# A two-layer decoder trunk: q, k and y1 transposed by VectorE in 32x32 blocks with a trip through DRAM, and the rotation moved from GpSimd to VectorE

## What is computed

```python
def moba_layer(x, norm_g, w_in, q_norm, k_norm, w_out):
    h = rms_norm(x, norm_g)
    q, k, v, z = jnp.split(h @ w_in, 4, axis=-1)
    q = rope(rms_norm(heads(q), q_norm))
    k = rope(rms_norm(heads(k), k_norm))
    v = heads(v)
    o = moba_attention(q, k, v).transpose(0, 2, 1, 3).reshape(B, S, D_INNER)
    return x + (o * jax.nn.silu(z)) @ w_out
```

## Time and profile before

| | us |
|---|---|
| median of 3 runs | 431.96 (431.88 to 432.15) |
| profiled execution | 431.83 |
| its span | 430.0 |
| PE busy | 423.4 (98%) |
| DVE busy | 284.7 (66%) |
| ACT busy | 231.0 (54%) |
| POOL busy | 131.1 (30%) |
| DMA moved | 75.25 MB, 175 GB/s |

### The profile page before, as it was taken

How to read it: one execution, slowest core, us unless ns; L and a number is a source line. 1 busy time by engine, 2 the same in 40 slices (tenths; PEclk the granted TensorE clock), 3 DMA queues, 4 the chain that set the end, 5 groups by cost and what they waited for, 6 DMA issues and landing times.

```text
span 430.0 us, 5669 instructions
## 1 busy us (share of the span) xinstructions
PE 423.4 (98%) x2214; PEld 362.7 (84%) x2214; DVE 284.7 (66%) x354; ACT 231.0 (54%) x406; POOL 131.1 (30%) x97
## 2 busy tenths in 40 slices
PE   8999999999999999999999999999999999999997
PEld 8979898988888888888788888888888888888885
DVE  3868898779885544356664798447983579836532
ACT  5743653535454443578448765477654786546310
POOL 0078000000000000089904595055940559300000
PEclk9999999999999999999999999999999999999999
DMA  8987669563655747336833667236672355731002
GB/s 260 386 298 241 209 219 365 190 201 122 197 194 173 219 134 221 125 89 214 292 99 99 185 183 228 91 100 193 196 215 84 101 191 195 243 110 39 2 0 98
DMA packets 38026, 75.25 MB, mean 175 GB/s; under 512 B 1648, under 2 KB 1776, under 8 KB 38000
## 3 DMA queue, kind: packets, MB, share of 16 engines
q1 hardware_dynamic: 37280, 73.83, 53.1%
q10 hardware_dynamic: 720, 1.07, 0.8%
HBM read 73.84 MB, written 1.05 MB: 174 GB/s over the span
## 4 chain that ended last, share of the span: by engine, by line
PE 85%; POOL 7%; DMA 2%; DVE 2%; SPq 1%; ACT 1%; issue 1%; DVEq 0%
PE acc L579 23%; PE acc L581 22%; PE acc L580 22%; PE aux L634 4%; POOL wide L326 3%; PE acc L624 3%; PE acc L623 3%; PE acc L621 3%; DMA raw<-in_w_in_dram 2%; PE aux L718 2%; POOL k_s L319 1%; PE aux L725 1%; SPq L232 1%; PE aux L736 1%; PE aux L737 1%; PE aux L717 1%
## 5 line engine op out<-in xcount | busy, mean ns | idle before, releaser
L816 DVE TENSOR_TENSOR w_lo<-raw,w_hi 128x2048 fp32r<-128x2048 f32 x65 | 160.1, 2469 | 54.9 <-ACT w_hi L349 54.8
L349 ACT ACTIVATE w_hi<-raw 128x2048 fp32r<-128x2048 f32 x64 | 122.1, 1917 | 36.7 <-PE acc L581 25.7
L579 PE MATMUL acc<-w_hi,hT_hi 128*128 128x512 f32 x320 | 127.8, 399 | 1.0 <-DVE w_lo L816 1.0
L581 PE MATMUL acc<-w_hi,hT_lo 128*128 128x512 f32 x320 | 124.9, 390 | 0.0
L580 PE MATMUL acc<-w_lo,hT_hi 128*128 128x512 f32 x320 | 124.6, 389 | 0.0
L579 PEld LDWEIGHTS acc<-w_hi,hT_hi 128*128 128x128 f32 x320 | 60.1, 188 | 12.9 <-DVE w_lo L816 1.4
L581 PEld LDWEIGHTS acc<-w_hi,hT_lo 128*128 128x128 f32 x320 | 60.0, 188 | 12.9
L580 PEld LDWEIGHTS acc<-w_lo,hT_hi 128*128 128x128 f32 x320 | 60.2, 188 | 11.7
L579 PE MATMUL acc<-w_hi,aT_hi 128*128 128x512 f32 x160 | 63.7, 398 | 0.0
L581 PE MATMUL acc<-w_hi,aT_lo 128*128 128x512 f32 x160 | 62.4, 390 | 0.0
L580 PE MATMUL acc<-w_lo,aT_hi 128*128 128x512 f32 x160 | 62.3, 389 | 0.0
(11 more groups left out here) (125 smaller groups left out, 569.7 us busy)
## 6 DMA issues: line engine op xcount, KB each, us to landing
raw<-in_w_in_dram SPq DMA_DIRECT2D x46, 1024.0 KB, 5.4
raw<-in_w_out_dram SPq DMA_DIRECT2D x16, 1024.0 KB, 5.0
raw<-in_w_pool_dram SPq DMA_DIRECT2D x4, 1024.0 KB, 5.7
raw<-in_w_in_dram SPq DMA_DIRECT2D x8, 256.0 KB, 7.5
wide<-in_xT_dram ACTq DMA_DIRECT2D x4, 256.0 KB, 7.0
xs<-in_x_dram SPq DMA_DIRECT2D x1, 1024.0 KB, 7.8
out_dram<-ysb SPq DMA_DIRECT2D x4, 256.0 KB, 2.1
wide<-in_table_dram SPq DMA_DIRECT2D x1, 256.0 KB, 9.0
```

The costliest lines, as they stand in the source:

```text
L349: act.activation(w_hi[:, slot, :], raw[:, slot, :], ACT.Copy).then_inc(hi_made, 1)
L579: pe.matmul(a, shi, whi, start=first and k == 0, stop=False)
L581: ins = pe.matmul(a, slo, whi, start=False, stop=last and k == GK - 1)
L816: dve.tensor_tensor(w_lo[:, slot, :], raw[:, slot, :], w_hi[:, slot, :].bitcast(F32), ALU.subtract).then_inc(w_split, 1)
```

## The change

TensorE no longer turns q, k, and the y1 of groups 0 to 2. In their place:

- The rotation is made by VectorE (`rope`): two products over half heads, one product and one sum, then `blocks`, one `dve.transpose` over 1024 columns that turns every 32x32 block in place. It stands after head 1's output for q and after w(4) for k. `y1_turn` is one such transpose after w(5).
- SyncE moves the blocks between the four bands of 32 partitions (`move_blocks`): one store of 128 x 1024 floats to DRAM, a wait until it has landed, and four fetches, one for each band, in runs of 256 floats. The three moves of a group stand in SyncE's list ahead of the loads 8g + 10, 8g + 12 and 8g + 13 (j = 3, 5, 6).
- GpSimd makes only the power (`norms`); the scaling of k is ScalarE's (`scale_k`).
- k is fetched straight into the place that `scores` reads, q is copied to its place by ScalarE (`lay_q`, after w(6)), and `y1_hi` reads what was fetched and stands ahead of `tanh_z`.
- VectorE's small product `minus_scale` for each head is made once per group by GpSimd (`minus_rstd`).

The last group's y1 is still turned by TensorE. In the diff below, hunks that only rename or declare are left out.

```diff
-        qT, kT = qkT[:, 0], qkT[:, 1]
+        qT = qkT[:, 0]
+        kT = qkT[:, 1].rearrange("p h s -> p (h s)").rearrange("p (a t h i) -> p t h a i", a=P // Q, t=TT, h=HPG)
...
+            def move_blocks(dst, blocks, between, times, stored, landed):
+
+                if times:
+                    sp.wait_ge(landed, MOVED * times)
+                sp.dma_start(between, blocks).then_inc(stored, 16)
+                sp.wait_ge(stored, 16 * (times + 1))
+                quadrants = between.rearrange("(a j) (b n) -> b j a n", j=Q, n=2 * P)
+                for b in range(P // Q):
+                    sp.dma_start(dst[b * Q:(b + 1) * Q, :].rearrange("j (a n) -> j a n", n=2 * P),
+                                 quadrants[b]).then_inc(landed, 16)
+
+            def flat(buf):
+                return buf.rearrange("p t n -> p (t n)")
+
+            def move_q(g):
+                sp.wait_ge(qk_blocked[0], g + 1)
+                move_blocks(flat(scratch[0]), flat(scratch[0]), between[0], g, qk_stored[0], qkT_landed[0])
+
+            def move_k(g):
+                sp.wait_ge(qk_blocked[1], g + 1)
+                sp.wait_ge(scores_ready, HPG * g)
+                move_blocks(flat(qkT[:, 1]), flat(scratch[1]), between[1], g, qk_stored[1], qkT_landed[1])
+
+            def move_y1(g):
+                sp.wait_ge(y1_blocked, g + 1)
+                move_blocks(flat(y1), y1_blocks, between[2], g, y1_stored, y1T_landed)
+
+            for i in range(8 * GROUPS + 8):
+                g, j = divmod(i - 7, 8)
+                if i >= 7 and g < GROUPS:
+                    if j == 3:
+                        move_q(g)
+                    if j == 5:
+                        move_k(g)
+                    if j == 6 and g > 0:
+                        move_y1(g - 1)
+                if i < 8 * GROUPS:
+                    g, j = divmod(i, 8)
                     src = w_in1_v[:, (j % 2) * GK:(j % 2 + 1) * GK, bass.ds((j // 2) * D_INNER + g * COLS, COLS)]
                     load(j % RING, src, N_L1 + 8 * g + j)
-            for i, (h, q) in enumerate(OUT1_ORDER):
-                load(i % RING, w_out1_v[:, q * GK:(q + 1) * GK, h * COLS:(h + 1) * COLS], N_OUT1 + i)
+                else:
+                    h, q = OUT1_ORDER[i - 8 * GROUPS]
+                    load(i % RING, w_out1_v[:, q * GK:(q + 1) * GK, h * COLS:(h + 1) * COLS], N_L1 + i)
...
+            def norms(g, i):
+
                 pool.wait_ge(squared[i], g + 1)
                 if i == 0 and g >= 2:
                     pool.wait_ge(exp_made, HPG * (g - 1))
-                scaled = pool.tensor_tensor(q_rstd[:, g % 2] if i == 0 else k_rstd[:, :, :], qk_mean[:, i],
-                                            minus_half[:, :].rearrange("p (t h) -> p t h", t=TT), ALU.pow)
+                ins = pool.tensor_tensor(q_rstd[:, g % 2] if i == 0 else k_rstd[:, :, :], qk_mean[:, i],
+                                         minus_half[:, :].rearrange("p (t h) -> p t h", t=TT), ALU.pow)
                 if i == 0:
-                    scaled.then_inc(qk_scaled, 1)
+                    chain.done(ins)
+                    pool.tensor_scalar(minus_rstd[:, g % 2], q_rstd[:, g % 2], -1.0, 1.0, ALU.mult,
+                                       ALU.mult).then_inc(qk_scaled, 1)
                 else:
-                    chain.done(scaled)
-                    for t in range(TT):
-                        ins = pool.tensor_tensor(v4[:, t], v4[:, t],
-                                                 k_rstd[:, t, :].unsqueeze(2).to_broadcast([P, HPG, HEAD_DIM]),
-                                                 ALU.mult)
-                    chain.done(ins)
-                for t in range(TT):
-                    for a, b in ((0, half), (half, 0)):
-                        tab = rope_tab[:, 2 * i + 1, t, a:a + half].unsqueeze(1).to_broadcast([P, HPG, half])
-                        ins = pool.tensor_tensor(s4[:, t, :, a:a + half], v4[:, t, :, b:b + half], tab, ALU.mult)
-                chain.done(ins)
-                for t in range(TT):
-                    tab = rope_tab[:, 2 * i, t, :].unsqueeze(1).to_broadcast([P, HPG, HEAD_DIM])
-                    ins = pool.tensor_tensor(v4[:, t], v4[:, t], tab, ALU.mult)
-                ins.then_inc(rope_parts[i], 1)
+                    ins.then_inc(k_rstd_made, 1)
...
-                    act.wait_ge(qk_turned[which], 2 * g)
+                    act.wait_ge(qk_blocked[which], g)
...
+                    if g > 0:
+                        act.wait_ge(qkT_landed[which], MOVED * g)
...
-            def qkT_out(g, i):
-                for b in range(2):
-                    act.wait_ge(qk_turned[i], 2 * g + b + 1)
-                    dst = (qT, kT)[i]
-                    act.activation(dst[:, 2 * b:2 * b + 2, :].rearrange("p h s -> p (h s)"), aux[2 * i + b][:, :],
-                                   ACT.Copy).then_inc(qkT_made[i], 1)
+            def scale_k(g):
+                act.wait_ge(k_rstd_made, g + 1)
+                for t in range(TT):
+                    for h in range(HPG):
+                        tile = k_s[:, t, h * HEAD_DIM:(h + 1) * HEAD_DIM]
+                        ins = act.activation(tile, tile, ACT.Copy, scale=k_rstd[:, t, h:h + 1])
+                ins.then_inc(k_scaled, 1)
...
+            def lay_q(g):
+                act.wait_ge(qkT_landed[0], MOVED * (g + 1))
+                act.wait_ge(scores_ready, HPG * g)
+                moved = scratch[0].rearrange("p t n -> p (t n)").rearrange("p (a t h i) -> p t h a i", a=P // Q, t=TT,
+                                                                           h=HPG)
+                for t in range(TT):
+                    act.activation(qT[:, :, t * P:(t + 1) * P].rearrange("p h (a i) -> p h a i", i=Q), moved[:, t], ACT.Copy).then_inc(qT_made, 1)
+
             def y1_hi(g):
+                act.wait_ge(y1T_landed, MOVED * (g + 1))
+                for t in range(TT):
+                    act.activation(y_tiles(aT_hi, g, t), y1T[:, :, t].rearrange("p a h i -> p h a i"),
+                                   ACT.Copy).then_inc(y_hi, 1)
+
+            def y1_hi_last():
                 for b in range(2):
-                    turned_hi(aT_hi, HPG * g + 2 * b, b, (y_turned, 8 + 2 * g + b + 1), y_hi)
+                    turned_hi(aT_hi, HPG * last + 2 * b, b, (y_turned, 8 + b + 1), y_hi)
...
                 w(4)
                 if attend:
                     probs_out(g - 1, 3)
+                scale_k(g)
                 w(5)
                 qkv_evacuate(g, 2, not attend)
                 w(6)
-                qkT_out(g, 0)
+                lay_q(g)
                 w(7)
+                if attend:
+                    y1_hi(g - 1)
                 tanh_z(g, not attend)
-                if attend:
-                    y1_hi(g - 1)
-                qkT_out(g, 1)
...
-                for i in range(2):
-                    pe.wait_ge(qkT_made[i], 2 * (g + 1))
-                if h < 2:
-                    pe.wait_ge(y_split, 8 + 2 * g)
+                pe.wait_ge(qT_made, TT * (g + 1))
+                pe.wait_ge(qkT_landed[1], MOVED * (g + 1))
+                if HPG * g + h < 2:
+                    pe.wait_ge(h_split, 4)
                 else:
                     pe.wait_ge(exp_made, HPG * g + h - 1)
                 s = aux[h % 2]
-                pe.matmul(s[:, 0:P], qT[:, h, 0:P], kT[:, h, 0:P], start=True, stop=True)
-                pe.matmul(s[:, P:3 * P], qT[:, h, P:SEQ], kT[:, h, :], start=True, stop=True).then_inc(scores_ready, 1)
+                pe.matmul(s[:, 0:P], qT[:, h, 0:P], kT[:, 0, h], start=True, stop=True)
+                pe.matmul(s[:, P:3 * P], qT[:, h, P:SEQ], kT[:, :, h], start=True, stop=True).then_inc(scores_ready, 1)
...
-            def turn_qk(g, i, first):
-                pe.wait_ge(roped[i], g + 1)
-                if first:
-                    pass
-                elif i == 0:
-                    pe.wait_ge(exp_made, HPG * g)
-                else:
-                    pe.wait_ge(y1_made, HPG * g)
-                turn((2 * i, 2 * i + 1), qk[i], qk_turned[i])
-
-            def turn_y1(g, after_q):
-                pe.wait_ge(y1_made, HPG * (g + 1))
-                if after_q is not None:
-                    pe.wait_ge(qkT_made[0], 2 * (after_q + 1))
-                turn((0, 1), y1, y_turned)
...
-                    if j == 6:
-                        turn_qk(g, 0, first)
-                    if j == 7:
-                        if not first:
-                            turn_y1(g - 1, g)
-                        turn_qk(g, 1, first)
...
-                    pe.wait_ge(y_split, 8 + k // 2 + 1)
+                    pe.wait_ge(y_split, 8 + (k // 2 + 1 if k >= HPG * last else 2 * (k // HPG) + 2))
...
-                dve.tensor_scalar(minus_scale[:, h, :], q_rstd[:, g % 2, :, h], -1.0, 1.0, ALU.mult, ALU.mult)
...
-                dve.wait_ge(y_turned, 8 + 2 * g)
+                dve.wait_ge(y_split, 8 + 2 * g)
...
```

(78 more changed lines are left out.)

7 lines of the change are left out of this document (4 added, 3 removed).

## The result

The changed kernel took **448.1 us** (median of 4 runs, 447.67 to 449.9) beside 432.01 before: a ratio of 1.038 with a 95% interval of 1.0364 to 1.0400. I had forecast 435.1 and a range up to 446. The sign was right, the size was not, and the time lies outside the range. The profiled execution took 447.67, its span 445.7, 15.7 more than the 430.0 before.

What follows compares the result with a forecast made beforehand. TensorE was taken as the bound, busy 219.3 of layer 1's 220 us. Stalls 3.6 x 2 + 5.0 + 1.2 = 13.4 us lost, 10.3 gained: +3.1 on 431.83, 434.9 profiled, 435.1 as median; range 424.5 to 446.

Steps and rivals of the forecast that it cites:

- the likeliest case: Whole kernel: stalls exceed the gain by queueing behind the weight load; 435.1 us, own range 433 to 440, chance 0.45.
- TensorE's gain: On TensorE: 11 turnings, 9.6 us, and group 0's wait of 0.7 us removed, 10.3 us in all.
- VectorE's order: VectorE after a group's last scores: ropes, splits, outputs, y1's transpose done at 48.1; holds nothing up, some 3.5 us spare.
- the moves of q and k hidden under other work: In each group: k's fetches land at 51.6, scores due at 55.9, so hidden with 4 us left.
- the chain from L to the exponentials: On ScalarE and VectorE: copy, tanh, y1's low part, maximum, exponentials of head 0, ready 6.4 us after y1's landing.
- L: Landing of y1's fetches, counted from a group's first matmul: 60.0 us forecast; the time is even at 59.0.
- Then SyncE issues a weight load at 49.1 (lands 54.5) and y1's store behind it: 55.9: SyncE's queue behind k's fetches, in us from a group's first matmul; y1's fetches then run from 56.0 to 60.0.
- my own queue rule: On SyncE's queue: a transfer lands 2.8 us later for each MB that stands ahead of it.
- the clock, which I had put into a rival: TensorE after idling: a clock restart can cost 2.0 us, three times, 441 us; chance 0.17 together with the longer chain.
- the second stall: On TensorE at head 0's values: ScalarE's late copies of the next q, 0.6 us late, twice, 1.2 us.
- the move is quick (1): y1's move: without queueing behind the weight load, or by overlap, it lands early; 423 us, middle 426, chance 0.30.
- The slow transpose (3): VectorE's block transposes take 2.5 us instead of 1.2; 440.5 us, 444 with slow fetches; chance 0.17 together with the clock.

Runs made afterwards that it cites:

- experiment 1: Changed kernel with y1's move ahead of the weight load that precedes it in SyncE's list; 430.4 us, ratio 0.9963 to the kernel before.
- experiment 2: Changed kernel with y1's high and low parts made one group later, moves and their order unchanged; 421.29 us, ratio 0.9765 to the kernel before.
- experiment 4: Changed kernel without y1's move: q and k moved through DRAM, y1 turned by TensorE as before; 424.0 us, ratio 0.9818 to the kernel before.
- experiment 7: Changed kernel with only y1 moved through DRAM, q and k turned by TensorE, rotation on VectorE; 428.58 us, ratio 0.9923 to the kernel before.
- experiment 9: Changed kernel with y1's move one weight load later in SyncE's list; 455.4 us, ratio 1.053 to the kernel before.
- Experiment 10: Changed kernel with y1 read a group later and y1's move right behind k's; 421.29 us, ratio 0.9751 to the kernel before.
- experiment 3: Changed kernel with 27 unused matmuls of 512 columns before head 0's turning in groups 1 to 3; 450.03 us, ratio 1.0437 to the kernel before.
- experiment 6: Changed kernel with y1's store and fetches started by GpSimd on its own queue; 446.36 us, ratio 1.0359 to the kernel before.
- experiment 8: Changed kernel with each fetch 128 partitions by 256 columns instead of 32 by 1024, blocks landing wrongly; 450.38 us, ratio 1.042 to the kernel before.

## Why the prediction was wrong

**What held.** The direction and its mechanism were the likeliest case's: y1's landing late behind a weight load, ScalarE waiting for it, head 0's exponentials queued behind, three waits of TensorE. Experiments 1, 2, 4, 7 and 9 each move that landing or its reader, and the time goes with it (430.4, 421.3, 424.0, 428.6, 455.4). TensorE's gain was right too (10.3 predicted, 10.7 with nothing waited for), as were VectorE's order, the cost of the transpose, the moves of q and k hidden under other work, and the chain from L to the exponentials.

**The step that failed: "Then SyncE issues a weight load at 49.1 (lands 54.5) and y1's store behind it: 55.9".** I had worked out that what stands ahead in the queue adds 1.4 us for each half MB, and used it for the stores of k and y1, but not for this load, which stands behind k's four fetches: I gave it the 5.4 of a median load. It took 8.2. With my own rule it would have been 6.8 and L 61.4; the rest, 1.4 us, I had no row for. (The rule's price was high, too: two loads issued one behind the other landed 2.1 us apart in experiment 9, where I had 2.8 us for each MB.) The store behind it then landed 1.3 us after it, as reckoned with 1.4 (in experiments 7 and 9 also 1.3 us after the last load ahead). So L was 63.3 instead of 60.0 in the first of the three groups. The loads took 2.8, 2.2 and 0.9 us more than 5.4, and the waits were 7.2, 6.4 and 6.5 us instead of 3.6, 3.6 and 5.0, that is 3.6, 2.8 and 1.5 more. Together that is 20.0 us of wait instead of 12.2: 7.8 of the 12.6 us by which the sum was short, and 5.9 of the 7.8 are the loads'. In the first group the other 0.8 us are the load's issue, 0.5 late, and TensorE's own date, 0.3 early (62.5 instead of 62.8).

**The second part: the clock, which I had put into a rival.** Experiment 10's span of 419.3 is the same work with no wait in the layer. What each kernel's span has above that, beyond its waits for the exponentials:

| kernel | span | waits | rest |
|---|---|---|---|
| after | 445.7 | 20.0 | 6.4 |
| y1 one load later | 453.8 | 29.6 | 4.9 |
| other fetches | 449.2 | 22.0 | 7.9 |
| GpSimd's queue | 444.0 | 18.0 | 6.7 |
| y1 first | 426.6 | 5.2 | 2.1 |

In the first four the rest is 5 to 8 us for three long waits, some 2 us each, and in the records it stands as matmuls at the lower of the two clock levels (1.2 GHz) for about 4 us behind each wait of the changed kernel. The windows behind the second and third wait in the changed kernel (for the first see experiment 3), and the one after it:

```profile
342.70:346.40 3.70, 3.69 (x11) 3.07 (x12) 1.84 (x6) 3.64 (x19) 0.00 (x0) 0.53 0.38 84
400.00:404.20 4.20, 4.20 (x12) 3.44 (x13) 4.03 (x7) 3.86 (x7) 0.00 (x0) 0.50 0.50 131
404.20:408.00 3.80, 3.80 (x20) 3.17 (x18) 0.00 (x0) 1.27 (x1) 0.00 (x0) 1.00 0.34 132
```

In 4.2 us 12 matmuls at 0.50, in the next 3.8 us 20 at 1.00. The three windows of the changed kernel at the lower level are 4.6, 3.7 and 4.2 us; half of their sum is 6.2 us, nearly all of the 6.4. The last row is another matter: in its profiled execution the clock stood at 1.00 from the first wait to the last, and of its 2.1 us 0.8 are short waits for later probabilities (`PE aux L787 <- ACT probsT L492: 0.8, 2, 0.4`); the other 1.3 us are open. I had priced the clock rightly, from the start of the kernel (2.0 us each, 6 in all), and given it too little chance: it follows from stalls of this length and is no alternative to them, and so it should have been a term of the likeliest sum. The two together: 3.1 + 7.8 + 6.4 - 1.2 (the second stall, which the changed kernel's list of waits doesn't have) - 0.4 (the better gain) = 15.7, the difference of the spans. The Trainium skill, page "TensorE: Matmul & The Clock Gate", Part 1, says that idling brings the lower level back; these runs show it, after waits of 6.4 to 7.2 us in the changed kernel, while after one of 0.87 us in experiment 3 the clock stood at 1.00.

**The range** ended at 446 because each case was widened alone. The middle case with the load by my own queue rule (L up by 1.4, so 4.2 us) and the clock (6 us) gives 435.1 + 4.2 + 6 = 445.3, and both hang on the same long wait. What the three loads took beyond that rule (1.4, 0.8 and -0.5 us) makes it 447.0, outside the range and near the 448.1 measured.

**The rivals.** That the move is quick (1) needed y1's store not to queue behind the load; experiment 1 made it so by order, and L fell by 6.1 us. Its other way, two transfers overlapping, was tried in experiment 6: they overlap and share the engines, and little is won (446.4 instead of 448.1). The slow transpose (3) is ruled out by 1.25 us. By the Trainium skill, page "DMA: Bandwidth & Descriptors", section "Anatomy of one DMA", the prediction had as an estimate 3.2 us for four fetches and L = 59.2. The trace doesn't agree: y1's four fetches took 4.2 us (273.13 to 277.32), as my 4.0 had it; and what made L 63.3, the longer load, was in neither sum.

**Left open.** Why the load behind k's fetches takes longer than 5.4 us, and how much. It isn't one number: it was 8.2, 7.6 and 6.3 us in the changed kernel, and 6.9, 7.6 and 7.6 in experiment 2, where the order in the queue is the same. Fetches ahead of a load don't suffice: in experiment 9 two loads stand behind y1's four fetches with nothing behind them, and took 5.5 and 6.4 us. A store behind it goes with a longer time even without fetches ahead: in experiment 7 the load ahead of y1's store had nothing ahead of it (the one before, issued at 252.5, had landed after 6.2 us, at 258.8) and yet took 6.4, with the store issued 1.2 us behind it. The trace's list of packets says the same: half of the load's packets had started 4.7 us after its issue in the changed kernel (263.61) and 4.4 in experiment 7 (259.38), against 3.5 in the load of experiment 9 with nothing behind it (276.99) and 3.4 in one with nothing ahead or behind in the kernel before (242.86). Two loads don't fit: 4.1 us with the store behind (381.92) and 4.1 with nothing behind (experiment 9, 338.16). So what the queue rule puts down to the bytes ahead may be in large part what stands behind; no run changes that alone, and the cause stays open. It isn't the fetches' 32 partitions (experiment 8). While the load at 263.61 was under way the engines moved 233 GB/s at a share of 0.81, so they were neither idle nor full. Short fetches from DRAM just written were not tried apart from others.

## What to carry to other kernels

A transpose through DRAM can be cheaper than TensorE's, if its result has a reader that can wait: the same moves cost 16 us when the reader stood in front of the exponentials and gained 10.6 when it stood a group later. Before moving a step onto a shared DMA queue, write down for each transfer what stands ahead of it and close behind it, and look at who is queued behind its reader on that reader's engine. When a forecast has TensorE idle for several microseconds, add the clock to the same case.

## What the runs showed of the hardware

- A block transpose of 128x1024 float32 on VectorE takes 1.25 us, as long as a sum of the same size (1.23).
- A store of 512 KB took 2.6 us for the first of a group, 4.8 behind two weight loads under way, a median of 8.3 (7.1 to 9.0) behind one load that itself was behind fetches, and of 10.4 behind two: 2.1 us for the further MB.
- Freeing a queue isn't free: on GpSimd's queue y1's store was quicker (4.25 us) and the fetches slower (7.1 instead of 2.8), with their first packet 4.0 us behind the issue and three loads beside them.
- Time saved on TensorE while a DMA chain sets the pace is given back in the next group (experiment 3); only what lies behind the last move is kept.
